# Four of eleven down-projection units as seven block products in place of eight

## The reference

```python
h = rms_norm(x, ffn_norm[i])
u = causal_depthwise_conv(h @ w_up[i], conv_w[i], conv_b[i])   # 256 x 5632
x = x + (jax.nn.silu(u[..., :D_FF]) * u[..., D_FF:]) @ w_down[i]      # D_FF = 2816
x = x + (p[i] @ ple_proj[i]) * jax.nn.sigmoid(x @ ple_gate[i])
```

## Time and profile before

| | |
|---|---|
| runs | 662.1, 662.16, 663.84 us, median 662.16 |
| profiled execution, first to last instruction | span 661.4 us; no other time is listed for it |
| TensorE busy | 653.2 us, 99% |
| VectorE, ScalarE, GpSimd busy | 67%, 64%, 61% |
| granted TensorE clock, mean | 1.000 of 2.4 GHz |
| transfers | 115.37 MB, 174 GB/s over the span |

### The profile page before, as it was taken

How to read it: one execution, slowest core, us unless ns; L and a number is a source line. 1 busy time by engine, 2 the same in 40 slices (tenths; PEclk the granted TensorE clock), 3 DMA queues, 4 the chain that set the end, 5 groups by cost and what they waited for, 6 DMA issues and landing times.

```text
span 661.4 us, 9574 instructions
## 1 busy us (share of the span) xinstructions
PE 653.2 (99%) x3792; PEld 562.9 (85%) x3792; DVE 441.5 (67%) x637; ACT 420.2 (64%) x633; POOL 402.8 (61%) x212
## 2 busy tenths in 40 slices
PE   8999999999999999999999999999999999999997
PEld 6988887888888888888889879878888888888885
DVE  5997778758989985003488777875798989810033
ACT  6669886677767675334474879756777777733332
POOL 5443510288888887987841353005888888889871
PEclk9999999999999999999999999999999999999999
DMA  9972125675565555553387421165555555555411
GB/s 318 363 257 64 66 105 158 201 236 191 191 190 192 192 191 190 191 191 107 108 283 248 156 100 64 65 207 176 192 190 191 191 192 191 191 191 190 160 33 63
DMA packets 74606, 115.37 MB, mean 174 GB/s; under 512 B 2369, under 2 KB 58433, under 8 KB 74305
## 3 DMA queue, kind: packets, MB, share of 16 engines
q1 hardware_dynamic: 73408, 111.95, 50.8%
q10 hardware_dynamic: 1152, 2.81, 1.2%
HBM read 113.70 MB, written 1.05 MB: 174 GB/s over the span
## 4 chain that ended last, share of the span: by engine, by line
PE 95%; DVE 2%; DMA 1%; ACT 0%; issue 0%; SPq 0%; ACTq 0%
PE ps L1516 24%; PE ps L963 15%; PE ps L964 14%; PE ps L965 14%; PE ps L1518 12%; PE ps L1109 1%; PE ps L1015 1%; DMA raw<-w_in 1%; PE ps L1135 1%; PE ps L1375 1%; PE ps L977 1%; PE ps L1050 1%; PE ps L1147 1%; DVE hn L2110 1%; PE ps L1539 1%; PE ps L1541 1%
## 5 line engine op out<-in xcount | busy, mean ns | idle before, releaser
L461 POOL TENSOR_TENSOR wl<-raw,wh 128x2048 fp32r<-128x2048 f32 (+1 forms) x74 | 332.6, 4499 | 86.3 <-ACT wh L590 86.3
L1516 PE MATMUL ps<-hT_hl,wh 128*128 128x512 f32 x688 | 238.6, 392 | 0.0
L590 ACT ACTIVATE wh<-raw 128x2048 fp32r<-128x2048 f32 (+1 forms) x100 | 180.6, 1809 | 77.0 <-PE ps L965 69.4
L1518 PE MATMUL ps<-hT_hl,wl 128*128 128x256 f32 x688 | 193.3, 281 | 0.0
L1516 PEld LDWEIGHTS ps<-hT_hl,wh 128*128 128x128 f32 x688 | 129.1, 188 | 28.2
L1518 PEld LDWEIGHTS ps<-hT_hl,wl 128*128 128x128 f32 x688 | 129.4, 188 | 0.0
L963 PE MATMUL ps<-wh,hT_hl 128*128 128x512 f32 (+1 forms) x216 | 79.7, 369 | 0.0
L965 PE MATMUL ps<-wh,hT_hl 128*128 128x512 f32 (+1 forms) x216 | 77.4, 359 | 0.0
L964 PE MATMUL ps<-wl,hT_hl 128*128 128x512 f32 (+1 forms) x216 | 77.3, 358 | 0.0
L2041 DVE TENSOR_TENSOR x<-x,ps 128x512 f32<-128x512 f32 x16 | 10.8, 686 | 99.1 <-PE ps L965 98.7
L448 POOL TENSOR_SCALAR st<-st 128x2 f32<-128x2 f32 (+3 forms) x22 | 6.5, 295 | 114.6 <-ACT lat L665 62.2
(11 more groups left out here) (321 smaller groups left out, 1182.9 us busy)
## 6 DMA issues: line engine op xcount, KB each, us to landing
raw<-w_up SPq DMA_DIRECT2D x44, 1024.0 KB, 5.1
raw<-w_down SPq DMA_DIRECT2D x22, 1024.0 KB, 4.9
raw<-w_in SPq DMA_DIRECT2D x16, 1024.0 KB, 9.9
raw<-w_o SPq DMA_DIRECT2D x6, 1024.0 KB, 5.1
raw<-ple_gate SPq DMA_DIRECT2D x6, 1024.0 KB, 4.9
raw<-w_in SPq DMA_DIRECT2D x4, 704.0 KB, 5.6
ng<-norm_gains ACTq DMA_DIRECT2D x2, 1024.0 KB, 6.6
raw<-w_o SPq DMA_DIRECT2D x4, 512.0 KB, 3.9
```

The costliest lines, as they stand in the source:

```text
L461: pool.tensor_tensor(wl[:, slot, 0:n], raw[:, slot, 0:n], w_high(u)[:, 0:n].bitcast(F32), ALU.subtract).then_inc(done, 1)
L590: act.activation(w_high(u)[:, c:n], raw[:, slot, c:n], ACT.Copy).then_inc(h_made, 1)
L1516: pe.matmul(both, high[:, c], hU_all[:, k].rearrange("p a n -> p (a n)"), start=k == 0, stop=False, skip_group_check=True)
L1518: mm = pe.matmul(o, wl[:, slot, c], hU_h[:, k, :], start=False, stop=k == KT - 1, skip_group_check=True)
```

## The change

Units 3, 5, 7 and 8 of each down phase (`SEVEN`) are computed with seven block products in place of eight (Strassen's scheme in Winograd's form). With A the 2 x 2 blocks of g for that unit (128 x 128 each) and B those of w_down (128 x 512), it needs four sums of A blocks (s1 to s4) and four of B blocks (T1 to T4), each split into high and low again. T1 (in place, in the slot) and T3 are made by transfers that GpSimd issues and that add to what stands in SBUF; T3 first needs a plain load of its first term, and the second is issued when that has landed. VectorE makes T2 and T4, the A sums, and all low parts of units 3 to 10, which GpSimd made before. GpSimd goes from the low part of unit 2 to the transfers, and then to the gate units. ScalarE rounds the sums. The buffers of the sums (`quarters`) lie on the up phase's activations and are two; the third and fourth of the seven-product units wait until the first and second are done.

Three of the seven products are added to PSUM banks 1 to 3 straight away; the other four gather in banks 4 to 7 over the four units. After unit 8, ScalarE copies banks 5 and 6, and VectorE adds the four up and into x in eight instructions, ahead of `add_to_x`.

```diff
+SEVEN = (3, 5, 7, 8)
+DVE_FROM = 3
 # gpsimd
-                for u in range(U_POOL, UNITS):
+                def weight_sums(i):
+                    u = U_DOWN + SEVEN[i]
+                    slot = u % DEEP
+                    b1, b2 = (w_down[layer][k * P:(k + 1) * P, :]
+                              for k in (2 * SEVEN[i], 2 * SEVEN[i] + 1))
+                    t3 = quarters[:, i % 2, 512:1024]
+                    unit_done(pool, layer, U_DOWN + SEVEN[i - 2] if i > 1 else U_DOWN - 1)
+                    pool.dma_start(t3, b1[:, 0:512]).then_inc(F["b12_landed"], 16)
+                    pool.wait_ge(raw_landed[slot],
+                                 (layer * (UNITS // DEEP) + u // DEEP + 1) * 16)
+                    pool.dma_start(raw[:, slot, 0:512], b1[:, 512:1024], accum_op=ALU.add
+                                   ).then_inc(F["t1_made"], 16)
+                    pool.wait_ge(F["b12_landed"], base["b12_landed"] + 16 * (i + 1))
+                    pool.dma_start(t3, b2[:, 0:512], accum_op=ALU.add
+                                   ).then_inc(F["t3_made"], 16)
+                    for name in ("t1_made", "t3_made"):
+                        pool.wait_ge(F[name], base[name] + 16 * (i + 1))
+                for u in range(U_POOL, U_DOWN + DVE_FROM):
+                    low(u)
+                for i in range(FEW):
+                    weight_sums(i)
+                for u in range(U_GATE, UNITS):
                     low(u)
 # scalar
+                def seven_high(i):
+                    u = U_DOWN + SEVEN[i]
+                    if i > 1:
+                        unit_done(act, layer, U_DOWN + SEVEN[i - 2])
+                    act.wait_ge(F["a_sums"], base["a_sums"] + i + 1)
+                    act.activation(a_high[:, i % 2, 0:3 * P], g_flat(SEVEN[i], True)[:, P:4 * P],
+                                   ACT.Copy)
+                    act.activation(a_high[:, i % 2, 3 * P:7 * P], g_flat(SEVEN[i], False), ACT.Copy
+                                   ).then_inc(F["a_rounded"], 1)
...
+                    act.wait_ge(F["w_sums"], base["w_sums"] + 2 * i + 2)
+                    act.activation(quarter_highs(i), quarters[:, i % 2], ACT.Copy
+                                   ).then_inc(F["w_rounded"], 1)
...
-                    if s:
+                    if s and s - 1 not in SEVEN:
                         product_high(s - 1)
...
-                for u in range(U_DOWN + 3, U_GATE + 1):
-                    high(u)
+                for s in range(DVE_FROM, STEPS):
+                    if s in SEVEN:
+                        act.wait_ge(F["t1_made"],
+                                    base["t1_made"] + 16 * (SEVEN.index(s) + 1))
+                    high(U_DOWN + s)
+                    if s in SEVEN:
+                        seven_high(SEVEN.index(s))
+                act.wait_ge(F["sevens_done"], base["sevens_done"] + 1)
+                for o, bank in ((both_sums, 6), (minus_both, 5)):
+                    act.activation(o, ps[:, bank, :], ACT.Copy).then_inc(F["sevens_copied"], 1)
+                high(U_GATE)
                 high(U_GATE + 1)
 # tensor, a unit of SEVEN in place of wide()
+                    pe.wait_ge(F["a_rest"], base["a_rest"] + i + 1)
+                    if i == 0:
+                        pe.wait_ge(F["conv_done"], base["conv_done"] + 4 * STEPS)
+                    low = wl[:, slot]
+                    product(4, a11, high, low, 1)
+                    product(3, a12, high, low, 3)
+                    product(2, s4, high, low, 2)
+                    product(5, s1, high, low, 0)
+                    pe.wait_ge(F["w_rest"], base["w_rest"] + i + 1)
+                    high, low = quarter_highs(i), quarter_sums(i)
+                    product(6, s2, high, low, 0)
+                    mm = product(7, s3, high, low, 1)
+                    if i == FEW - 1:
+                        mm.then_inc(F["sevens_done"], 1)
+                    product(1, a22, high, low, 2).then_inc(w_used, 1)
 # vector, after the last product_low
+                for s in range(DVE_FROM, STEPS):
+                    if s in SEVEN:
+                        weight_sums(SEVEN.index(s))     # waits t3_made; T2, T4: 512 columns each
+                        act_sums(SEVEN.index(s))        # s1 to s4: 128 columns each
+                    down_low(s)                         # 2048 columns
+                    if s in SEVEN:
+                        act_rest(SEVEN.index(s))        # 384 and 512 columns
+                        weight_rest(SEVEN.index(s))     # 1536 columns
+                dve.wait_ge(F["sevens_copied"], base["sevens_copied"] + 2)
+                parts = [x[:, t, c] for t, c in map(quarter, range(4))]
+                chained(tt(both_sums, both_sums, ps[:, 4, :], ALU.add))
+                chained(tt(minus_both, minus_both, both_sums, ALU.subtract))
+                tt(parts[2], parts[2], minus_both, ALU.add)
+                chained(tt(both_sums, both_sums, ps[:, 7, :], ALU.add))
+                chained(tt(parts[1], parts[1], both_sums, ALU.add))
+                chained(tt(minus_both, minus_both, ps[:, 7, :], ALU.subtract))
+                tt(parts[0], parts[0], minus_both, ALU.add)
+                chained(tt(parts[3], parts[3], ps[:, 4, :], ALU.add))
                 add_to_x("down_done", U_GATE - 1, "x_mlp")
```

More of the change, by code:

```diff
@@ L75, with eights @@
 STEPS = FT // 2
+SEVEN = (3, 5, 7, 8)
+FEW = len(SEVEN)
+DVE_FROM = 3
+def eights(s):
+    return s - sum(f < s for f in SEVEN)
 def unit_up(s, half):
@@ L205, in build @@
         hT = sb("hT", [P, KT, SEQ])
+        with nc.sbuf_tensor("quarters", [P, 2, 1536], F32) as quarters:
+            pass
         hT_hl = sb("hT_hl", [P, KT * 2 * SEQ + UP_AT], F32R)
@@ L210, in build @@
         sb("hT_edge", [P, 32])
+        with nc.sbuf_tensor("g_plain", [P, 2 * STEPS, 512], F32) as g_plain:
+            pass
         gT_h = sb("gT_h", [P, 2, 2, SEQ], F32R)
@@ L233, in build @@
         pT_h = sb("pT_h", [P, 2, SEQ], F32R)
+        with nc.sbuf_tensor("a_high", [P, 2, 7 * P], F32R) as a_high:
+            pass
         ng = sb("ng", [P, 2 * D])
@@ L297, in g_low, with g_flat, quarter_sums, quarter_highs @@
             return gT_l[:, s] if s < EARLY else g_late[:, 1, s - EARLY]
+        def g_flat(s, first):
+            n = 2 * EARLY + s - EARLY
+            return g_plain[:, n if first else n + STEPS - EARLY]
+        def quarter_sums(i):
+            return hT_hl[:, (i % 2) * 1536:(i % 2 + 1) * 1536]
+        def quarter_highs(i):
+            return (proj_h, pt_r)[i % 2][:, 0:1536]
+        both_sums, minus_both = (qk_swa[:, 2 * a:2 * a + 2, :].rearrange("p k n -> p (k n)")
+                                 for a in range(2))
         def mixed(high, g):
@@ L367, in ffn_lows @@
         def ffn_lows(layer, u):
-            return layer * (UNITS - U_POOL) + (u + 1 - U_POOL)
+            n = STEPS - DVE_FROM
+            return layer * (UNITS - U_POOL - n) + (u + 1 - U_POOL - (n if u >= U_GATE else 0))
         @block.sync
@@ L901, in _ @@
                     high(unit_up(s, 0) + 3)
-                    if s:
+                    if s and s - 1 not in SEVEN:
                         product_high(s - 1)
-                    if s > 1:
-                        act.wait_ge(F["g_low"], base["g_low"] + s - 1)
+                    if s > 1 and s - 2 in SEVEN:
+                        act.wait_ge(F["prod"], base["prod"] + s - 1)
+                    elif s > 1:
+                        act.wait_ge(F["g_low"], base["g_low"] + eights(s - 1))
                     taps(s, 0)
@@ L1525, in _, with down_seven, product @@
                 pe.wait_ge(F["conv_done"], base["conv_done"] + 4 * (STEPS - 1))
+                def down_seven(i):
+                    s = SEVEN[i]
+                    slot, high = unit(U_DOWN + s)
+                    raw_a, sums_a = (g(s).rearrange("p k n -> p (k n)") for g in (g_high, g_low))
+                    rounded = a_high[:, i % 2]
+                    a = [(rounded[:, n * P:(n + 1) * P],
+                          raw_a[:, (n + 1) * P:(n + 2) * P] if n < 3 else
+                          sums_a[:, (n - 3) * P:(n - 2) * P]) for n in range(7)]
+                    a11, a22, a12, s1, s2, s3, s4 = a
+                    def product(bank, act, b_h, b_l, n):
+                        c = slice(n * 512, (n + 1) * 512)
+                        own = bank >= 4
+                        return split_product(ps[:, bank, :], *act, b_h[:, c], b_l[:, c],
+                                             own and i == 0, own and i == FEW - 1)
+                    pe.wait_ge(F["a_rest"], base["a_rest"] + i + 1)
[13 more added lines that the diff above has]
+                    product(1, a22, high, low, 2).then_inc(w_used, 1)
                 for s in range(STEPS):
-                    pe.wait_ge(F["g_low"], base["g_low"] + s + 1)
+                    if s in SEVEN:
+                        down_seven(SEVEN.index(s))
+                        continue
```

(39 more changed lines are left out.)

18 lines of the change are left out of this document (14 added, 4 removed).

## The result

The changed kernel takes **712.67 us** (median of 4 runs, 711.63 to 713.87) against 662.33 for the kernel before on the same chip (4 runs, 662.1 to 663.84): ratio 1.0758, 95% interval 1.074 to 1.0776. It is slower, as forecast, but by 50 us where 16.8 were forecast, and above the range. The profiled span is 710.2 us against 661.4, 48.8 more.

What follows compares the result with a forecast made beforehand. TensorE, busy 99% of 661.4 us, was taken as the bound. Two layers of +3.1 us (stalls less saved matmuls) and +5.3 us (late closing additions) add 16.8 us: 678.2 span, 679.0 us forecast, range 667 to 691.

Steps and rivals of the forecast that it cites:

- The saving: Down phase: four units lose 3 of 24 matmuls each on TensorE, 2.72 us a layer, 5.44 us in all.
- VectorE's unit: VectorE's work for one seven-product unit of the down phase: 7.42 us against TensorE's 4.76.
- The end of the phase: Closing additions after unit 8 hang behind GpSimd's gate subtractions, delaying the transposes of x: +5.3 us a layer.
- five of them read two operands from SBUF: Of VectorE's eight closing additions, five were said to have the form that hangs beside GpSimd, 4.64 us for 0.69.
- the term S: Time of two serial 256 KB transfers, plain then adding, before VectorE can start a unit's sums: taken as 6.5 us.
- the upper end: Top of the range for the two serial transfers, about 10 us, since a 1 MB load runs beside them.
- the same walk: Unit-by-unit timing of the down phase: stalls of 3.4 us at unit 3, 2.4 at unit 8; +3.1 us a layer.
- The left-out term: TensorE's clock: matmuls were priced at 0.2267 us, with granted clock 1.00; no slowing after stalls was forecast.
- The sum: Forecast loss per layer, 3.1 us in the down phase plus 5.3 at its end; twice that is 16.8 us.
- the one that said 689: Rival: from unit 5 on, GpSimd's transfer preparation waits for VectorE, 5 us more a layer; 18 in 100.
- d: Forecast time at which VectorE starts unit 3's sums in layer 0: 262.6.
- The sums in time: Rival: transfers done by 258, TensorE keeps its saving, no hang: 4.8 us gained, 657.4; 6 in 100.

Runs made afterwards that it cites:

- the last version: Changed kernel with sums' transfers issued early, one between two of GpSimd's last low parts, and GpSimd's gate low parts held until after the closing additions: 657.74 us.
- the first experiment: Changed kernel, with GpSimd's gate low parts waiting until VectorE's last two-operand closing addition is done: 701.82 us.

## Why the prediction was wrong

- **The saving** of 2.72 us a layer was right, and the last version shows 2.41 of it in each layer (61.51 - 59.10); a longer step of 0.42 us into unit 8 takes 0.2 of the rest.
- **VectorE's unit**: 7.42 us forecast, 273.84 - 266.50 = 7.34 measured. Right.
- **The end of the phase**: +5.3 us a layer forecast, 3.6 + 1.6 = 5.2 measured; two additions hang for 4.40 and 4.23 us, as said, and the first experiment takes it away, 5.4 a layer. The mechanism was right, the closeness of the number partly luck: the last addition ended 16.2 us after unit 8 (315.41 to 331.65), not 16.8, so x came 4.4 us later than before, and slower transposes, which the forecast didn't have, made up the rest. Its "five of them read two operands from SBUF" is a misreading of the change: four do, and the other four read one from PSUM.
- **The failed step is the term S.** "I take S = 6.5. Ends: 2 x 2.0 = 4.0, and 2 x 4.9, about 10": measured 10.45 to 12.75, beyond the upper end. By unit 3 the stall is 8.4 us instead of 3.4. Unit 7 was to be in time; with S = 12.75 from a buffer that came free at 280.92 it stalls 3.8. At unit 8, 3.2 against 2.4, GpSimd issued only at 294.20, since it still waited for unit 7's pair. The runs without adding and of transfers by themselves say what S at unit 3 is made of: 2 x 3.2 = 6.4 for two plain loads alone, 9.3 - 6.4 = 2.9 for what runs beside them, 11.6 - 9.3 = 2.3 for adding (1.4 of it is there alone too). The 2.9 are a difference; how they divide between SyncE's loads and T1's own transfer wasn't tried. The sum took its price from SyncE's transfers, those of w_down in a phase whose DMA engines were busy 0.50 of the time, where in the change it is 0.90 while VectorE waits, and scaled it with bytes; the 1 MB loads beside were named for the upper end alone. Nor did the range hold that end: by the same walk S = 10 makes the stalls 6.8 and 5.8 us and the time about 693, past 691. (By the Trainium skill, "DMA: Bandwidth & Descriptors", Anatomy of one DMA, 2.0 us plus the bytes over 436 GB/s make 2.6 us for 256 KB, an estimate; 3.2 were measured alone with its wait, and 4.9 for the first plain load in place. By that rule the forecast would have been further off.)
- **The left-out term** is the clock. The forecast kept 1.00 throughout, as in the earlier trace rows; the granted clock fell to the 1.2 GHz level after the stalls of 8.4 and 3.8 us, 6.0 us in layer 0, and in the transposes.
- **The sum** of layer 0 was 8.4 and became 24.0. Of the 15.6 between, 5.0 + 3.8 + 0.8 = 9.6 are S in the stalls and 6.0 the clock behind these; the end is -0.1.
- **The rivals**: the one that said 689 had slower transfers, but from VectorE's instructions and only from unit 5 on; its cause is refuted. (Its own terms land unit 8's sums at d + 32.0, not 32.5, and give about 688.) "The sums in time" at 657.4 names what the last version does, 657.74, but that needs another order of the transfers and GpSimd's gate work held back, so not this change.

## What to carry to other kernels

Price a transfer that is new to a queue by what runs beside it, not by a row from a quieter stretch, and issue it where its landing isn't waited for: here, with GpSimd's gate work held back in both, the same sums cost 40 us when they are issued at their unit's turn (701.82) and gain 4 us when they are issued early (657.74). A stall of TensorE can cost more than its length, as the clock may fall behind it. And a two-operand instruction of VectorE that meets one of GpSimd's waits for whole instructions of it, so what is put between one engine's instructions (here a DMA issue) decides how long the other waits.

## What the runs showed that was not expected

- A 256 KB transfer issued by GpSimd takes 3.2 us alone, 4.6 when it adds; 6.6 and 7.9 beside 1 MB loads on another queue. GpSimd is busy some 0.55 us with the issue of a plain one (0.8 for the first in a stretch) and some 0.9 with an adding one.
- VectorE's two-operand instruction of 0.69 us hung for 10.63 us when two of GpSimd's subtractions ran without a pause between them, against 4.64 beside one.
- Gaps of nearly the same length left the clock differently. In the change, ahead of unit 8, a gap of 3.44 us from start to start was followed by 1.00 throughout the unit in layer 0; after one of 3.46 us in layer 1 it was 1.00 up to 660.70 and 0.51 from there to 664.10.
